# Attention with the probabilities stationary in the value product, and the maxima from a rough pass

## What is computed

```python
def block_attention(q, k, v):
    B, T = q.shape[:2]
    nb = T // Q_BLOCK
    qb = q.reshape(B, nb, Q_BLOCK, N_KV_HEADS, Q_PER_KV, HEAD_DIM).transpose(1, 0, 3, 4, 2, 5)
    scale = HEAD_DIM ** -0.5

    def one_block(qblk):
        s = jnp.einsum('bkgqd,bskd->bkgqs', qblk, k).astype(jnp.float32) * scale
        p = jax.nn.softmax(s, axis=-1).astype(v.dtype)
        return jnp.einsum('bkgqs,bskd->bkgqd', p, v)

    o = lax.map(one_block, qb)
    return o.transpose(1, 0, 4, 2, 3, 5).reshape(B, T, N_Q_HEADS * HEAD_DIM)
```

## Time and profile before

| | |
|---|---|
| Median of 3 runs | 3546.38 us (3546.01 to 3548.62) |
| The profiled execution's own time | 3547.59 us |
| Its span in the profile | 3545.8 us |
| TensorE (PE) busy | 3171.3 us, 89% |
| VectorE (DVE) busy | 1878.6 us, 53% |
| ScalarE (ACT) busy | 1671.7 us, 47% |
| GpSimd (POOL) busy | 388.6 us, 11% |
| DMA queues | 393.69 MB, 111 GB/s |

### The profile page before, as it was taken

One profiled execution on the slowest core, in us unless ns is written; L12 is line 12 of the kernel. 1 busy time (PEld: TensorE's weight loads), 2 busy tenths in 40 slices (PEclk: granted clock), 3 DMA queues, 4 the chain that ended last, 5 costly groups with the idle time before them and its releaser, 6 DMA issues. The chain is left out here.

```text
span 3545.8 us, 60756 instructions
## 1 busy us (share of the span) xinstructions
PE 3171.3 (89%) x21856; PEld 2900.2 (82%) x21856; DVE 1878.6 (53%) x3485; ACT 1671.7 (47%) x3239; POOL 388.6 (11%) x400
## 2 busy tenths in 40 slices
PE   6999994759999999999699756999999999999991
PEld 6788883748888888888588645999999999999991
DVE  2222226548888888888533365545455445545443
ACT  2222220547777777777434202455455544455442
POOL 0333333500000000000000000010010000110001
PEclk9999997869999999999799855999999999999996
DMA  5121113410000000000244204565565555665545
GB/s 217 43 80 60 67 66 116 140 42 25 27 27 27 27 27 27 27 27 27 81 147 150 83 0 132 174 192 185 179 198 184 183 187 179 188 193 181 181 130 220
DMA packets 307599, 393.69 MB, mean 111 GB/s; under 512 B 13808, under 2 KB 263872, under 8 KB 306496
## 3 DMA queue, kind: packets, MB, share of 16 engines
q1 hardware_dynamic: 293680, 338.64, 28.9%
q0 software_dynamic: 10240, 35.66, 4.4%
q10 hardware_dynamic: 3600, 18.35, 1.3%
HBM read 318.68 MB, written 74.06 MB: 111 GB/s over the span
## 5 line engine op out<-in xcount | busy, mean ns | idle before, releaser
L2304 DVE TENSOR_TENSOR e_w_lo<-e_raw,e_w_hi 128x2048 fp32r<-128x2048 f32 x192 | 440.1, 2292 | 490.4 <-ACT e_w_hi L2246 490.4
L92 PE MATMUL e_ps<-e_x_hi,e_w_hi 128*128 128x272 f32 x2048 | 602.1, 294 | 5.5 <-issue 5.5
L94 PE MATMUL e_ps<-e_x_hi,e_w_lo 128*128 128x272 f32 x2048 | 593.8, 290 | 0.0
L93 PE MATMUL e_ps<-e_x_lo,e_w_hi 128*128 128x272 f32 x2048 | 590.1, 288 | 0.0
L2246 ACT ACTIVATE e_w_hi<-e_raw 128x2048 fp32r<-128x2048 f32 x192 | 366.1, 1907 | 163.7 <-DMA e_raw<-in_w_gate 159.3
L1470 DVE TENSOR_TENSOR a_pT_lo<-a_ps_t,a_pT_hi 128x512 fp32r<-128x512 f32 (+1 forms) x648 | 368.0, 601 | 139.5 <-ACT a_pT_hi L1368 139.2
L1368 ACT ACTIVATE a_pT_hi<-a_ps_t 128x512 fp32r<-128x512 f32 (+1 forms) x648 | 319.6, 532 | 185.1 <-PE a_ps_t L1238 180.5
L92 PEld LDWEIGHTS e_ps<-e_x_hi,e_w_hi 128*128 128x128 f32 x2048 | 386.1, 189 | 7.1 <-issue 5.5
L93 PEld LDWEIGHTS e_ps<-e_x_lo,e_w_hi 128*128 128x128 f32 x2048 | 386.9, 189 | 0.0
L94 PEld LDWEIGHTS e_ps<-e_x_hi,e_w_lo 128*128 128x128 f32 x2048 | 385.8, 188 | 0.0
L1443 DVE TENSOR_REDUCE a_mx<-a_ps_s 128x1 f32<-128x896 f32 (+2 forms) x392 | 346.1, 890 | 26.8 <-PE a_ps_s L1228 26.8
(11 more groups left out here) (269 smaller groups left out, 5478.2 us busy)
## 6 DMA issues: line engine op xcount, KB each, us to landing
e_raw<-in_w_gate SPq DMA_DIRECT2D x64, 1024.0 KB, 5.2
e_raw<-in_w_up SPq DMA_DIRECT2D x64, 1024.0 KB, 5.2
e_raw<-in_w_down SPq DMA_DIRECT2D x64, 1024.0 KB, 5.2
a_wm<-in_w_mod SPq DMA_DIRECT2D x32, 512.0 KB, 4.0
s_ret<-p_pr SPq DMA_DIRECT2D x17, 768.0 KB, 3.6
m_raw<-in_w_in ACTq DMA_DIRECT2D x8, 1152.0 KB, 7.1
o_cT<-s_ct SPq DMA_DIRECT2D x17, 512.0 KB, 4.7
s_x<-o_x SPq DMA_DIRECT2D x17, 512.0 KB, 4.9
```

What stands on the lines that cost most here:

```text
L92: nc.tensor.matmul(out, w_hi, x_hi, start=first, stop=False)
L93: nc.tensor.matmul(out, w_hi, x_lo, start=False, stop=False)
L94: return nc.tensor.matmul(out, w_lo, x_hi, start=False, stop=last)
L2304: nc.vector.tensor_tensor(w_lo[n % RING][:, :, :], raw[n % RING][:, :, :], w_hi[n % RING][:, :, :].bitcast(F32), ALU.subtract).then_inc(w_ ...
```

## The change

The work of attention is ordered by slots. A slot is one query tile `i` and one key head `v` with its four query heads, 512 query columns together; 32 slots for the latent tiles, then two small ones for the context tile. In a slot the 17 key tiles go in nine pairs (`j`), the last with one tile.

- The scores are computed with the keys stationary: the result has keys on the partitions and 512 queries in the columns, one key tile per PSUM bank, three banks. Two products per tile: high part of the keys (twice, over the queries' high and low part), then low part of the keys (64 rows) against the queries' high part. A 65th row of the second product holds ones on the key side and the negative maximum on the query side (`qM`), which subtracts the maximum inside the product.
- So the maximum must be known before. A rough pass computes the scores of the **next** slot once more with the keys' high part alone, queries stationary: 16 pieces of 512 keys and one piece of four 128-key products; VectorE reduces each piece, and `tops` joins them. The 4 x 65-column transposes (`turn_top`) bring the maxima into a row, ScalarE copies it with the sign turned.
- The exponentials come out already with keys on the partitions, so no transposes of probabilities. ScalarE rounds a pair of tiles (`high`, 1024 elements), VectorE subtracts (`low`, one key tile at a time, from SBUF) with a maximum between two of them.
- In the value product the probabilities are stationary (128 queries) and the values move: two columns of ones, high part, low part (130 columns) for the high probabilities, and 66 columns for the low ones. 17 x 4 x 2 products a slot. The ones give the row sums; the result has queries on the partitions, so the folding goes. ScalarE copies the sums, VectorE inverts the denominators, GpSimd adds the halves and multiplies.
- PSUM: one bank for queries, modulation, maxima and output (`ps_m`), two for the rough pass, three for scores, two for the sums.
- Key preparation: ScalarE rounds one key tile ahead of the copy; the low part is 64 wide and not doubled.

The diff, cut to its core. Constants, the products, and TensorE's slot:

```diff
-BANK_W = [448, 448, 448, 448, KEY_TILES * P - 4 * 448]
-SEGS = [(0, 2), (2, 2), (4, 1)]
...
+PAIRS = (KEY_TILES + 1) // 2
+QCOLS = QPK * P
+PARTS = (KEY_TILES - 1) * P // QCOLS
+PIECES = PARTS * QPK + 1
+PIECES_IN = [2, 2, 2, 2, 2, 2, 2, 3, 0]
+ONES = 2
+VCOLS = ONES + 2 * HD
+QUADS = NKV * NT
+RING = 3
...
+            def rough(i, v, n):
+
+                if n == 0:
+                    pe.wait_ge(emptied, use_of_queries(i, v) + 1)
+                if not (first_slot(i, v) and n < 2):
+                    pe.wait_ge(max_ok, piece(i, v, n) - 1)
...
+            def scores(i, v, j, t):
...
+                elif c >= 3:
+                    pe.wait_ge(exped, n - 2)
...
+                nc.tensor.matmul(to[:, :], keys[:, v, src * P:(src + 1) * P], qT[v][:, :], start=True, stop=False)
+                nc.tensor.matmul(to[:, :], keys_lo[:, v, src * P:(src + 1) * P], qM[v][:, :], start=False, stop=True)\
+                    .then_inc(scored, 1)
+
+            def value(i, v, j, t):
+
+                n = pair(i, v, j)
+                if t == 0:
+                    pe.wait_ge(hi_ok, n + 1)
+                    pe.wait_ge(lo_ok, n + 1)
+                    if j == 0 and not first_slot(i, v):
+                        pe.wait_ge(o_kept, 2 * quad(i, v))
...
+                for c in range(QPK):
+                    q = slice(c * P, (c + 1) * P)
+                    nc.tensor.matmul(out_block(c), p_hi[:, place(i, v, j), t, q], vals[:, src, v, :],
+                                     start=first and c in (0, 3), stop=False, skip_group_check=True)
+                    ins = nc.tensor.matmul(out_block(c)[:, 0:ONES + HD], p_lo[:, place(i, v, j), t, q], vals[:, src, v, 0:ONES + HD],
+                                           start=False, stop=last, skip_group_check=True)
...
+            turn_queries(0, 0)
+            for n in range(PIECES):
+                rough(0, 0, n)
+            turn_top(0, 0)
+
+            def slot(i, v):
+                last, ahead = before(i, v), following(i, v)
+                at = 0
+                for j in range(PAIRS):
+                    todo = list(range(at, min(at + PIECES_IN[j], pieces_of(ahead[0]))))
+                    at = at + PIECES_IN[j]
+                    if j == 0:
+                        if not first_slot(i, v):
+                            for t in range(2):
+                                value(*last, PAIRS - 2, t)
+                        turn_queries(*ahead)
+                    for t in tiles_of(i, j):
+                        scores(i, v, j, t)
+                        if todo and j and t == 0:
+                            rough(*ahead, todo.pop(0))
+                    if j == PAIRS - 1:
+                        turn_top(*ahead)
+                    if j == 1 and not first_slot(i, v):
+                        value(*last, PAIRS - 1, 0)
+                    for t in range(2):
+                        if j >= 2:
+                            value(i, v, j - 2, t)
+                        if todo:
+                            rough(*ahead, todo.pop(0))
+                    if j == 2:
+                        modulation(i, v)
+                    if j == 5 and not first_slot(i, v):
+                        turn_out(*last)
```

ScalarE's slot:

```diff
+            def slot(i, v):
+                last, ahead = before(i, v), following(i, v)
+                for j in range(PAIRS):
+                    if j == 0:
+                        keep_queries(*ahead)
+                    if j == 2 and not first_slot(i, v):
+                        keep_sums(*last)
+                    if j == 6 and not first_slot(i, v):
+                        keep_out(*last)
+                    for t in tiles_of(i, j):
+                        exps(i, v, j, t)
+                    if j == PAIRS - 1:
+                        keep_top(*ahead)
+                    high(i, v, j)
+                    if j == 2 and v == 0:
+                        queries_hi(i + 1)
```

VectorE's slot:

```diff
+            def slot(i, v):
+                last, ahead = before(i, v), following(i, v)
+                at = 0
+                for j in range(PAIRS):
+                    todo = list(range(at, min(at + PIECES_IN[j], pieces_of(ahead[0]))))
+                    at = at + PIECES_IN[j]
+                    if j == 3:
+                        keep_modulation(i, v)
+                    if j == 3 and not first_slot(i, v):
+                        denominators(*last)
+                    if j == 0:
+                        if not first_slot(i, v):
+                            low(*last, PAIRS - 1, 0)
+                        copy_queries(*ahead)
+                    if todo:
+                        maxima(*ahead, todo.pop(0))
+                    if j == PAIRS - 2:
+                        for n in todo:
+                            maxima(*ahead, n)
+                        todo = []
+                        tops(*ahead)
+                    for t in range(2):
+                        if j:
+                            low(i, v, j - 1, t)
+                        if todo:
+                            maxima(*ahead, todo.pop(0))
+                    if j == 4 and v == 0:
+                        queries_lo(i + 1)
```

More of the change, by code:

```diff
@@ L1144, in body @@
[L1144 to L1165 removed]
+                    sp.wait_ge(q_lo_ok, i)
@@ L1188, in key_tile @@
                 if not known(h, off, 0) and not known(h, off, 1):
[L1189 to L1194 removed]
+                    pe.wait_ge(k_kept, 2 * (i - 1))
@@ new lines, in body @@
+            def body(i):
+                for v in range(NKV):
+                    slot(i, v)
+            slots(pe, body)
+            for t in range(2):
+                value(NT - 1, 1, PAIRS - 2, t)
+            turn_queries(NT, 1)
+            scores(NT, 0, 0, 0)
+            value(NT - 1, 1, PAIRS - 1, 0)
+            rough(NT, 1, 0)
+            value(NT, 0, 0, 0)
+            turn_out(NT - 1, 1)
+            turn_top(NT, 1)
+            scores(NT, 1, 0, 0)
+            value(NT, 1, 0, 0)
@@ L1414, in _ @@
+            def body(i):
+                for v in range(NKV):
+                    slot(i, v)
+            slots(act, body)
+            keep_queries(NT, 1)
+            exps(NT, 0, 0, 0)
+            high(NT, 0, 0)
+            keep_sums(NT - 1, 1)
+            keep_out(NT - 1, 1)
+            keep_top(NT, 1)
+            keep_sums(NT, 0)
+            exps(NT, 1, 0, 0)
+            high(NT, 1, 0)
+            keep_out(NT, 0)
+            keep_sums(NT, 1)
+            keep_out(NT, 1)
         @block.vector
@@ L1531, in _ @@
+            def body(i):
+                for v in range(NKV):
+                    slot(i, v)
+            slots(dve, body)
+            low(NT - 1, 1, PAIRS - 1, 0)
+            copy_queries(NT, 1)
+            low(NT, 0, 0, 0)
+            maxima(NT, 1, 0)
+            tops(NT, 1)
+            denominators(NT - 1, 1)
+            denominators(NT, 0)
+            low(NT, 1, 0, 0)
+            denominators(NT, 1)
             second_gain()
```

653 lines of the change are left out of this document (276 added, 377 removed).

## The result

The changed kernel takes 4256.8 us (median of four runs, 4256.4 to 4261.6) against 3547.2 us (3546.0 to 3548.6) for the kernel before: ratio 1.200, 95% interval 1.198 to 1.202. Slower was forecast, but 3594 us; the range ended at 3655. The profiled execution took 4261.6 us, with a span of 4259.8.

What follows compares the result with a forecast made beforehand. TensorE was taken to bound attention: 28.9 us of work and 2.8 of waits made a 31.7 us slot against 29.6, +67 over 32 slots; with the stage's ends +47.7, so 3594 us, range 3510 to 3655.

Steps and rivals of the forecast that it cites:

- What the change does to TensorE: TensorE's work for a slot of four heads: 28.9 us against 26.8 before, bounds 22.9 and 31.0.
- Loads set the pace of the value products: Value products on TensorE start 0.11 us apart, paced by loading weights, not columns: 14.2 us a slot.
- The rival of quicker loads: Short value products with new weights pace at up to 0.06 us: slot 26.7, time 3434 us; chance 0.05.
- the 3492 us by the 81 ns of the Trainium skill: At 81 ns per load and product of 128 columns, the slot would be 28.5 us; no separate chance.
- The seams: TensorE's waits at three places in a slot, together 3.1 us, taken as 2.8 for overlap.
- the top: First seam: TensorE idles 0.9 us before the maxima's transposes, waiting for VectorE's last maximum and reduction.
- the low parts: First seam: pair 6's value product waits 0.9 us more for low parts VectorE forms after the reduction.
- the third piece: Second seam, a slot's start: the third rough piece waits 0.4 us for query copies and the first maximum.
- the sums: Third seam: a slot's first value product waits 0.9 us for ScalarE to copy the last sums.
- Ends of the stage: Attention outside the slots: first scores after 55.4 us, key tiles 1.9 apart, tail less 2.5, context tile plus 19.5.
- GpSimd's work and the weight loads hidden: GpSimd's two operations and a 512 KB weight block per slot cost nothing, covered by 29 us of TensorE's work.
- Slower, with 0.68: Chance 0.68 that the changed kernel is slower by over 0.2%; faster had 0.26, within 0.2% had 0.06.

Runs made afterwards that it cites:

- e3: Changed kernel with each 512-column rough product made three times over and nothing removed; 4086.3 us, ratio 1.151 to the kernel before.
- c3: Changed kernel, 130 and 66 columns kept, with the last rough piece two pairs sooner and the sums copied out one pair sooner; 4204.3 us, ratio 1.185.
- a1: Changed kernel with both value products widened to 256 columns, extra sums never read, sum blocks 256 apart; 3668.6 us, ratio 1.034.
- d1: Changed kernel with 130 columns in both value products, sums laid out as in a1, rough piece and sums copy earlier; 4108.5 us, ratio 1.158.
- d4: Kernel before with each 256-column value product split in two, the high one moving 128 columns, the low one 66; 3745.8 us, ratio 1.056.
- e1: d4 with probability transposes made as float32r products with the identity, probabilities rounded to float32r; 3905.9 us, ratio 1.101.
- e2: Control of e1: d4 with the same rounding of probabilities, transposes left in float32; 3746.0 us, ratio 1.055.
- c1: a1 with the last rough piece two pairs sooner and the sums copied before the second pair's high parts; 3650.5 us, ratio 1.029.
- c2: c4 with low probabilities and their values in bfloat16, and the earlier seam work of c1; 3807.3 us, ratio 1.070 without the slowest run.
- c4: Changed kernel with only the high value products widened to 256 columns, low ones at 66, sums as in a1; 3779.3 us, ratio 1.065.

## Why the prediction was wrong

**The step that failed** is the first one: the earlier trace rows showed a granted clock of 1.00 and every term of the sum was priced at it, as if the clock belonged to the kernel and not to the work. "What the change does to TensorE" took away 68 transposes for each four heads and put in 136 narrow products, and no rival asked what that does to the clock. The only clock below 1.00 in the text was that of the drain.

At the full clock the sum was right, as far as an estimate can say. A run of eight value products was to take 0.82 us and takes 0.81 (median of those at the full clock in the changed kernel and in e3); the run of 32 was to take 3.5, and c3 has one at 3.57. From a1's slot of 34.03 us, whose runs take 0.954 and 3.88 us, the changed kernel's slot at the full clock is estimated as 34.03 - 13 x (0.954 - 0.81) - (3.88 - 3.57) = 31.85 us; the forecast was 31.7. Measured are 52.4. So some 20.5 us a slot, 660 us over 32 slots, are the clock, and the miss is 663.

**Point by point.**
- Loads set the pace of the value products, at 0.11 us: right at the full clock (0.223 us a pair in the changed kernel, and the same with 130 and 192 columns). The rival of quicker loads fell. So did the 3492 us by the 81 ns of the Trainium skill (TensorE: Matmul & The Clock Gate, Back-to-back issue gap).
- The seams, 2.8 us a slot: right in place and nearly in size, where the clock lets them show. In a1 the starts lie 1.04 us apart at the top, 0.88 at the low parts, 0.48 at the third piece and 0.79 at the sums, where the usual distances are 0.24, 0.11, 0.24 and 0.24: together 2.4. In the changed kernel the profile shows 0.7 us a slot.
- Ends of the stage: first scores 56.0 us after the first load (forecast 55.4), key tiles 1.87 us apart (1.9), the rest behind the 32 slots 17.9 (17.0). The terms that the text gives for the first scores, 58.6 - 17 + 11.6 + 4.4, come to 57.6, not 55.4; the 2.2 us between them have no reason in it.
- ScalarE's and VectorE's operations last what was said (0.60, 0.69, 0.69 us); that they would be 70% and 78% busy was wrong with the slot (41% and 44% of the long stretch).
- GpSimd's work and the weight loads hidden: right, nothing waits for them.
- Slower, with 0.68: by the same estimate the changed kernel would have been slower at the full clock too, by some 50 us (forecast 47). But of the 710 us measured, 660 have a reason that the text did not have, so that the sign came out right is no proof of its sum.

The forecast's own signs of being wrong told it at once: starts 0.2 us apart were named as wrong, and that is what the timeline shows between 1037.90 and 1039.46.

What stays open: why closing the seams lowered the clock at 130 columns (d1), and by what measure transposes and wide products count. It is not the mean number of columns per time: counted from the program, d4 moves some 39,300 columns (values, transposes and scores) for four heads in 35.4 us at a clock of 0.96, and the changed kernel some 39,400 in a slot, which at the full clock would be 31.85 us, so its stream is the denser one. The rough pass even brings as many columns as the transposes took away, 8,704, but as products of 512. How the narrow products are grouped may matter: the changed kernel has them in runs of eight between 512-column products and in one run of 32, d4 in runs of 8 to 24 between scores and transposes. No run changed the grouping alone. That the transposes stream for all of their 0.11 us is inferred from the shorter loads and from e1 against e2, not seen in a record. And no run has the changed kernel's 130 and 66 columns with the sums laid out as in a1; what is shown with that held fixed is the step from 130 and 130 (0.74) to 256 and 256 (1.00).

## What to carry to other kernels

A duration read from a trace holds at the clock of its row, and the clock belongs to the mix of work: when a change swaps wide products and float32 transposes for narrow ones that are paced by their loads of weights, price the new mix at both levels, 1.2 and 2.4 GHz, and give the lower one a rival. A TensorE that is 98% busy with no waits can be running at half speed; look at the granted clock before the busy share. And where the clock is what limits the kernel, more columns, even columns that nobody reads, can be worth hundreds of microseconds.

## What the runs showed of the hardware

- TensorE was busy 98.6% of 1666 us and its granted clock was 0.57. The Trainium skill (TensorE: Matmul & The Clock Gate, HAM oscillation) tells of the clock falling over idle gaps of TensorE, while it waits for transfers. The runs here don't test such waits for transfers: inside the slots the longest idle gap of any run is 0.9 us (c1, d1), and 0.4 in the changed kernel. What the runs add is that the clock can be low with hardly a gap, and 1.00 with waits of up to 0.6 us at every seam (a1).
- Added work made a kernel faster: 32 more 512-column products a slot, 170 us less; 64 more float32 transposes, 92 us less.
- The same 128x128 transpose has a load of 0.144 us in float32 (e2) and of 0.234 us as a float32r product at e1's mixed clock (0.19 in its stretches at 1.00). At the full clock both kinds start 0.11 us apart; swapping the one for the other cost 160 us, nearly all of it through the clock.
- A bfloat16 product of 66 columns beside a float32r one of 256 made the pair longer: 0.244 us against 0.230 with both in float32r (c2, c4).
